# A hybrid mLSTM and sliding-window attention step: an earlier release for the score banks, and another order on VectorE ahead of h

## The chip, the cores and the metric

The kernel runs on one core of a Trainium2 chip. A core has five engines with an instruction stream each: TensorE (PE in the profile, with its weight loads as PEld), VectorE (DVE), ScalarE (ACT), GpSimd (POOL) and SyncE (SP), which here only issues DMAs. They meet by semaphores. The metric is the time of one execution in microseconds, median of several runs.

## What is computed

One layer for 1024 prompt tokens and 8 x 8 sample tokens: an RMS norm, one input projection, two groups of heads beside each other, one output projection, a norm and a residual. Cut to what matters here:

```
proj = rms(x, g_pre) @ w_in            # split into qa ka va za | qm km vm om zm ig fg
# attention: 8 query heads, 2 key heads of 64, window 128, a sink per head
s = einsum(qa, ka) * 64**-0.5 + bias
p = softmax(concatenate([s, sink]))[..., :-1]
a_out = einsum(p, va) * silu(za)
# mLSTM: 4 heads of 128, chunks of 128 tokens; D and g are exponentials of the gates
S = einsum(qm, km) * D
num = einsum(S, vm) + g * einsum(qm, C)
den = sum(S) + g * einsum(qm, n)
h = num / maximum(abs(den), exp(-m))
C, n = decay * C + einsum(w, km, vm), decay * n + einsum(w, km)
m_out = sigmoid(om) * rms(h, g_mh) * silu(zm)
y = x + rms(concatenate([a_out, m_out]) @ w_out, g_post)
```

## The kernel before

All operands are fp32; the large products are split into a high and a low part, so that one sub-tile of the input projection is 24 matmuls (8 slices of the inner dimension, three products each, L551). The projection has 25 tiles of 128 output columns (`ka`, four each of `qa`, `km`, `qm`, `za`, `om`, `zm`), each cut into three sub-tiles of 368, 368 and 352 tokens: 75 sub-tiles. They use two PSUM banks in turn. ACT evacuates each (`evac`), and after some of them splits the next weight tile: `w_hi` on ACT, then `w_lo` on POOL (attention) or DVE (mLSTM).

The small work is laid between the sub-tiles by hand. Every engine runs the same loops, `it` counting the sub-tile, and the order within an iteration is the order of the code. There is no scheduler.

**Attention stage** (24 iterations, the sub-tiles of `km` and `qm`). Unit `u` is half of the heads of one block of 128 queries, u = 0 to 15; unit 16 is all sample tokens. In iteration `it` PE computes `scores(it)` (32 matmuls, L602, into banks 0 and 1), then 24 matmuls of the projection, and in odd iterations `values((it - 3) // 2)` (L628), for which it waits for `pT_done`. DVE does `denominators(it - 1)`, `band_transpose(it - 2)` (writes `pT`, L1253) and `score(it)`: L1227 reads the two banks, scales and adds the bias and writes `prob`; L1238 to L1241 take the row maxima, put in the sink, negate, and write `sd`, which lets semaphore `scored` go up. ACT waits for `scored` and takes the exponentials of `prob` (L954), then evacuates the sub-tile. POOL multiplies by `rden` (L1523), ahead of the transpose. `step` is a helper: its instruction raises `dve_step`, and DVE waits for that before it issues the next.

**mLSTM stage** (12 iterations, the sub-tiles of `za`). Unit 0 is the sample tokens, units 1 to 8 are the prompt's chunks. PE in iteration `it`: `h_transposes(it - 2)` (L749), `numerator(it - 1)` and `state_update(it - 1)` (L702 to L714), 7 matmuls of the projection, `m_scores(it)` (L678), `sample_inter`, 7 matmuls, `sample_round` (L738), `k_transposes(it)` (L687), 10 matmuls. `h_transposes` waits for both `h_done` and `sd_done`. DVE: the mask `DT` (L1285), `hT_evac` (L1372), `h_denominator`, `state`, `inter_second` in even iterations, `h_mean_square` (L1357, L1358), `h_scale` (L1364, writes `hs`), `q_gate` (L1293, `qmT` times the exponentials `Gt`, both in SBUF), `sd_mul` (L1276, the scores in PSUM times `DT`, writes `SD`), the split `w_lo` in every third iteration, and the update of the sample state `Cs`. Between L1358 and L1364 POOL computes the factor `hf` in three small operations (L1553, L1484 with a power of -0.5, L1555) and then `vmk` (L1545).

Of the kernel before, what the change touches and what calls it, by code (L numbers as in the profile page):

```python
# [22 lines left out]
ALU = mybir.AluOpType  # L23
# [11 lines left out]
AH, KVH, HD = 8, 2, 64  # L35
# [9 lines left out]
BAND = WIN + PQ  # L45
# [56 lines left out]
def build(nc, i, o):  # L102
# [12 lines left out]
    def sb(name, shape, dt, offset):  # L115
        return nc.alloc_sbuf_tensor_at(name, shape, dt, offset=offset)
# [19 lines left out]
    k = [at["K"]]  # L136
# [52 lines left out]
    bias_0 = sb("bias_0", [P, AH, BAND], F32, GI + 10496)  # L189
    kcT = sb("kcT", [P, DEC_B, KEYS_S], F32, GI + 10496)  # L190
    vc = sb("vc", [P, DEC_B, KV_W], F32, GI + 14848)
    bias_p = sb("bias_p", [P, AH, BAND], F32, GI + 18944)
# [56 lines left out]
    ps = nc.alloc_psum_tensor("ps", [P, 8, 512], F32)  # L249
    sems = {}  # L250

    def s(name):
        if name not in sems:
            sems[name] = nc.alloc_semaphore(name)
        return sems[name]
# [12 lines left out]
    def wait(eng, name, value):  # L268

        if value > 0:  # L270
            eng.wait_ge(s(name), value)
# [26 lines left out]
    def unit_tokens(u):  # L298

        return (NC, T_P, T_S) if u == 0 else (u - 1, P * (u - 1), P)  # L300
# [181 lines left out]
    def _(pe):  # L482
# [91 lines left out]
        for c in range(NTILE):  # L574
            _, n = x_cols(c)
            last = nc.tensor.transpose(ps[0:PQ + MH, c // 4, (c % 4) * P:(c % 4) * P + n], gates[0:n, c, 0:PQ + MH], ident[0:n, 0:n])
# [9 lines left out]


        def scores(u):
            wait(pe, "scored", u)
            if u == 0:  # L590
                wait(pe, "proj_free", S_P2 - 2)
                wait(pe, "cols_done", 1)
            if u < 2 * NC:
                blk, pair = u // 2, u % 2
                if u == 0:
                    wait(pe, "kpad_ready", 1)
                for g in range(2):
                    for kv in range(KVH):
                        rows = slice(kv * HD, (kv + 1) * HD)
                        for a in range(4):  # L600
                            q0 = blk * P + PQ * a
                            last = mm(ps[PQ * a:PQ * (a + 1), kv, g * BAND:(g + 1) * BAND], qaT[rows, 2 * pair + g, q0:q0 + PQ],  # L602
                                      kaT_pad[rows, q0:q0 + BAND], start=True, stop=True)
            else:
                wait(pe, "qs_ready", 1)
                pe.wait_ge(s("kc_ld"), 32)
                for b in range(DEC_B):
                    r = 32 * (b % 4)
                    for kv in range(KVH):
                        rows = slice(kv * HD, (kv + 1) * HD)  # L610
                        last = mm(ps[r:r + 32, kv, (b // 4) * KEYS_S:(b // 4 + 1) * KEYS_S], qs[rows, b, :], kcT[rows, b, :],
                                  start=True, stop=True)
            last.then_inc(s("qk_done"), 1)
# [478 lines left out]
    def _(dve):  # L1092
        V = nc.vector
        step = Step(dve, "dve_step")
        TT, TS, STT, CP = V.tensor_tensor, V.tensor_scalar, V.scalar_tensor_tensor, V.tensor_copy
# [85 lines left out]
        for dst, bias, q in ((ib, bgi, 0), (fb, bgf, PQ)):  # L1181
            last = TS(dst[:], ps[q:q + MH, 0:3, :].rearrange("p b t -> p (b t)")[:, 0:T], bias[q:q + MH, 0:1], None, ALU.add)
# [11 lines left out]
        for b in range(DEC_B):  # L1194
            c0 = T_P + DEC_T * b
            last = V.tensor_tensor_scan(out=rd[:, c0:c0 + DEC_T], data0=rc[:, c0:c0 + DEC_T], data1=ib[:, c0:c0 + DEC_T],
                                        initial=m0T[:, b:b + 1], op0=ALU.add, op1=ALU.max)
# [19 lines left out]
        def score(u):  # L1217

            wait(dve, "qk_done", u + 1)
            wait(dve, "pT_done", u - 1)  # L1220
            b = u % 2
            if u == 0:
                dve.wait_ge(s("bias_ld"), 48)
            if u < 2 * NC:
                heads = slice(4 * (u % 2), 4 * (u % 2) + 4)
                p = prob[:, b, :, :]
                step(STT(out=p.rearrange("p (v g) k -> p v g k", v=KVH), in0=ps[:, 0:2, 0:2 * BAND].rearrange("p v (g k) -> p v g k", g=2),  # L1227
                         scalar=float(HD) ** -0.5, in1=(bias_0 if u < 2 else bias_p)[:, heads, :].rearrange("p (v g) k -> p v g k", v=KVH),
                         op0=ALU.mult, op1=ALU.add))
                sink = sink_p[:, heads]  # L1230
            else:
                for kv in range(KVH):
                    last = STT(out=prob_s[:, 2 * kv:2 * kv + 2, :], in0=ps[:, kv, 0:2 * KEYS_S].rearrange("p (a k) -> p a k", a=2),
                               scalar=float(HD) ** -0.5, in1=bias_s[:, kv:kv + 1, :].broadcast_to([P, 2, KEYS_S]),
                               op0=ALU.mult, op1=ALU.add)
                step(last)
                p, sink = prob_s[:], sink_s[:]
            step(V.tensor_reduce(mx[:, b, :], p, AX_X, ALU.max))  # L1238
            step(TT(mx[:, b, :], mx[:, b, :], sink, ALU.max))  # L1239
            TS(nmx[:, b, :], mx[:, b, :], -1.0, None, ALU.mult)  # L1240
            TT(sd[:, b, :], sink, mx[:, b, :], ALU.subtract).then_inc(s("scored"), 1)  # L1241
# [29 lines left out]
        def sd_mul(u):  # L1271
            _, _, n = unit_tokens(u)
            wait(dve, "d_done", u + 1)
            wait(dve, "s_done", u + 1)
            wait(dve, "num_done", u - 1)
            TT((SD if u else SDs)[0:n, :, :], ps[0:n, 1, 0:MH * n].rearrange("p (h t) -> p h t", h=MH), DT[0:n, :, 0:n], ALU.mult)\  # L1276
                .then_inc(s("sd_done"), 1)

        def mask_weights(u):
            _, _, n = unit_tokens(u)  # L1280
            dve.wait_ge(s(f"r_ld{u % 3}"), 32 if u == 0 else 16 * (u // 3 + (2 if u % 3 == 0 else 1)))
            wait(dve, "kw_done", u)
            m = causal if u else causal_s
            r1 = Gt[:, u % 3, :, :] if u else Gt[0:T_S, 0, 2:4, :].rearrange("p a (h t) -> p (a h) t", t=T_S)
            TT(DT[0:n, :, 0:n], r1, m[:].unsqueeze(1).broadcast_to([n, MH, n]), ALU.min).then_inc(s("mask_done"), 1)  # L1285
# [45 lines left out]
        def inter_second(r):  # L1331
            wait(dve, "it_done", r + 1)
            wait(dve, "it_evac", r)
            part = ITs[:, r // 2, :]
            STT(out=part, in0=ps[:, 4, IT0:IT0 + W1], scalar=inter_msk[:, 1:2], in1=part, op0=ALU.mult, op1=ALU.add)\
                .then_inc(s("it_evac"), 1)

        def num_view(n):
            return ps[0:n, 2:4, 0:2 * W1].rearrange("p b (h v) -> p b h v", v=W1)
# [20 lines left out]
        def h_scale(u):  # L1360
            _, _, n = unit_tokens(u)
            v = H_ORDER.index(u) + 1
            wait(dve, "hf_ready", v)
            TT(hs[0:n, :, :].rearrange("p (b h) v -> p b h v", b=2), num_view(n)[:, :, :, 0:MD],  # L1364
               hf[0:n, :].rearrange("p (b h) -> p b h", b=2).unsqueeze(3).broadcast_to([n, 2, 2, MD]), ALU.mult)\
                .then_inc(s("h_done"), 1)

        def hT_evac(u):
            _, off, n = unit_tokens(u)
            v = H_ORDER.index(u) + 1  # L1370
            wait(dve, "hT_done", v)
            TT(qmT[:, :, off:off + n], ps[:, 1, 0:MH * n].rearrange("p (h t) -> p h t", h=MH),  # L1372
               gmh[:].unsqueeze(2).broadcast_to([P, MH, n]), ALU.mult).then_inc(s("hT_evac"), 1)

        def splits(sub):
            for n in PLAN.get(sub, []):
                split_lo(dve, V, n)

        for it in range(S_P4 - S_P3):
            if it <= NC:  # L1380
                mask_weights(it)
            if it >= 3:
                hT_evac(it - 2 if it <= NC + 2 else 0)
            done = None
            if 2 <= it <= NC + 2:
                done = it - 1 if it <= NC + 1 else 0
                h_denominator(done)
            if 2 <= it <= NC + 1:
                state(it - 1)
            if 1 <= it <= N_ROUND and it % 2 == 0:  # L1390
                inter_second(it - 1)
            if done is not None:
                h_mean_square(done)
                h_scale(done)
            if it <= NC:
                q_gate(it)
                sd_mul(it)
            if it == 0:
                sample_extras()
            if it >= 1:  # L1400
                splits(S_P3 + it - 1)
            if 1 <= it <= N_ROUND:
                sample_state(it - 1)
            if it < N_ROUND:
                sample_n(it)
# [56 lines left out]
        p = NTILE - 1  # L1462
# [7 lines left out]
        for q in range(2):  # L1470
            wait(dve, "yg_done", q + 1)
            STT(out=ys[q], in0=ys[q], scalar=stat[:, NTILE + p:NTILE + p + 1], in1=x_res[:, p % 2, 512 * q:512 * (q + 1)],
                op0=ALU.mult, op1=ALU.add).then_inc(s("y_ready"), 1)
# [208 lines left out]
```

## Time and profile before

| | us |
|---|---|
| median of 3 runs (573.79 to 574.02) | 573.85 |
| the profiled execution | 573.66 |
| its span in the trace | 571.8 |
| PE busy | 550.1 |
| DVE busy | 249.3 |
| ACT busy | 200.0 |
| POOL busy | 132.9 |
| idle time of PE in 148 to 262 us, put down to DVE | 1.9 |
| idle time of PE in 262 to 375 us, ahead of L749 | 1.7 |

The span runs from the first to the last recorded instruction; the execution is some 1.9 us longer. In the rows further down a timeline line gives start, duration, engine, line of the kernel, operation, output and inputs, the number of instructions merged, and in brackets the idle time of that engine just before and the instruction that ended it. The stages by time: norm, transposes and token-major projection up to about 85 us, gates and first tiles to 148, attention to 262, mLSTM to 375, gates and the rest of the projection, then the output projection from about 470.

### The profile page before, as it was taken

How to read it: one execution, taken by the hardware profiler on the slowest of the kernel's cores; microseconds unless marked ns; L12 is line 12 of the kernel's file. 1: busy time of each engine (PE TensorE's matmuls, PEld its weight loads, DVE VectorE, ACT ScalarE, POOL GpSimd, SP SyncE). 2: the span in 40 equal slices, each digit the busy share in tenths (PEclk: the TensorE clock that was granted, in tenths of full speed). 3: DMA queues.
4: the chain of work that ended last, by engine and by line, in shares of the span. 5: the costliest groups of instructions: out<-in, count | busy, mean ns of one | idle time of the engine just before them, and what ended most of it. 6: DMA issues, size and time to landing. Idle time of an engine off the chain costs nothing.

```text
span 571.8 us, 10440 instructions
## 1 busy us (share of the span) xinstructions
PE 550.1 (96%) x4354; PEld 507.0 (89%) x4354; DVE 249.3 (44%) x468; ACT 200.0 (35%) x542; POOL 132.9 (23%) x148
## 2 busy tenths in 40 slices
PE   2999999999999999999999999999999999999996
PEld 2999999999988889899888888899999998888874
DVE  3743214910456666611366757335324327052223
ACT  3352223223354545432565464244332224011011
POOL 3511021112323434331112121235422220011001
PEclk9999999999999999999999999999999999999999
DMA  8422006131142122014233320411122315044231
GB/s 312 147 76 91 1 2 211 77 112 38 38 134 62 62 63 83 6 36 105 64 93 112 89 79 20 111 49 63 37 75 77 108 37 185 0 148 147 102 101 55
DMA packets 34166, 48.72 MB, mean 85 GB/s; under 512 B 3888, under 2 KB 25456, under 8 KB 34104
## 3 DMA queue, kind: packets, MB, share of 16 engines
q1 hardware_dynamic: 25544, 43.80, 23.5%
q10 hardware_dynamic: 8576, 4.26, 2.9%
q8 instruction: 34, 0.56, 0.4%
q14 instruction: 12, 0.10, 0.1%
HBM read 40.48 MB, written 8.56 MB: 86 GB/s over the span
## 4 chain that ended last, share of the span: by engine, by line
PE 74%; DVE 14%; ACT 6%; DMA 2%; issue 2%; POOL 1%; SPq 0%; ACTq 0%; DVEq 0%; POOLq 0%
PE ps L551 37%; PE ps L490 8%; PE ps L491 8%; PE ps L492 8%; ACT prob L954 4%; DVE mx L1238 2%; DVE prob L1227 2%; DVE pT L1253 2%; PE ps L510 1%; PE ps L702 1%; DVE mx L1239 1%; DMA g_pre_b<-in_g_pre 1%; PE ps L714 1%; PE ps L704 1%; PE ps L495 1%
## 5 line engine op out<-in xcount | busy, mean ns | idle before, releaser
L551 PE MATMUL ps<-x_hl,w_hi 128*128 128x368 f32 (+1 forms) x1200 | 300.0, 330 | 0.8 <-ACT qaT L887 0.6
L551 PEld LDWEIGHTS ps<-x_hl,w_hi 128*128 128x128 f32 x1200 | 210.0, 188 | 7.5 <-issue 5.9
L551 PE MATMUL ps<-x_hl,w_lo 128*128 128x368 f32 (+1 forms) x600 | 197.0, 328 | 0.0
L551 PEld LDWEIGHTS ps<-x_hl,w_lo 128*128 128x128 f32 x600 | 112.7, 188 | 0.1
L329 POOL TENSOR_TENSOR w_lo<-w_raw,w_hi 128x1024 fp32r<-128x1024 f32 x14 | 33.7, 2406 | 86.1 <-ACT w_hi L864 86.1
L490 PE MATMUL ps<-wt_hi,x_hl 128*128 128x324 f32 x128 | 41.8, 327 | 1.6 <-DVE x_hl L1114 1.4
L954 ACT ACTIVATE prob<-prob,nmx 128x160 f32<-128x160 f32 x64 | 26.6, 417 | 46.6 <-DVE sd L1241 46.6
L492 PE MATMUL ps<-wt_hi,x_hl 128*128 128x324 f32 x128 | 40.8, 318 | 0.0
L491 PE MATMUL ps<-wt_lo,x_hl 128*128 128x324 f32 x128 | 40.7, 318 | 0.0
L1573 POOL TENSOR_TENSOR qmT<-qmT,sg 128x368 f32<-128x368 f32 (+1 forms) x24 | 25.0, 1041 | 57.8 <-DVE sg L1426 36.4
L1523 POOL TENSOR_TENSOR prob<-prob,rden 128x640 f32<-128x640 f32 x16 | 20.1, 1254 | 63.8 <-DVE rden L1247 63.8
L877 ACT ACTIVATE sg<-ps 128x368 f32<-128x368 f32 (+1 forms) x24 | 11.4, 474 | 63.6 <-PE ps L551 63.6
L1456 DVE SCALAR_TENSOR_TENSOR y_out<-ps,stat,g_post_b 128x1024 f32<-128x1024 f32 x7 | 9.0, 1283 | 50.2 <-POOL stat L1484 50.2
L864 ACT ACTIVATE w_hi<-w_raw 128x1024 fp32r<-128x1024 f32 x25 | 26.3, 1051 | 12.0 <-DMA w_raw<-in_w_in_tiles 12.0
L1088 ACT ACTIVATE junk<-ps 128x1024 f32<-128x1024 f32 x7 | 7.2, 1026 | 60.0 <-PE ps L492 60.0
L490 PEld LDWEIGHTS ps<-wt_hi,x_hl 128*128 128x128 f32 x128 | 25.1, 196 | 2.6 <-DVE x_hl L1114 1.8
L490 PE MATMUL ps<-wah,a_hl 128*128 128x512 f32 x64 | 25.3, 395 | 0.0
L491 PE MATMUL ps<-wal,a_hl 128*128 128x512 f32 x64 | 25.3, 395 | 0.0
L492 PE MATMUL ps<-wah,a_hl 128*128 128x512 f32 x64 | 25.3, 395 | 0.0
L491 PEld LDWEIGHTS ps<-wt_lo,x_hl 128*128 128x128 f32 x128 | 25.0, 195 | 0.0
L491 PE MATMUL ps<-wbl,m_hl 128*128 128x512 f32 x64 | 25.0, 390 | 0.0
L490 PE MATMUL ps<-wbh,m_hl 128*128 128x512 f32 x64 | 24.9, 390 | 0.0
(221 smaller groups left out, 802.9 us busy)
## 6 DMA issues: line engine op xcount, KB each, us to landing
w_raw<-in_w_in_tiles SPq DMA_DIRECT2D x25, 512.0 KB, 3.6
x_raw<-in_x_prompt SPq DMA_DIRECT2D x8, 512.0 KB, 3.9
w_raw<-in_w_out_tiles SPq DMA_DIRECT2D x8, 512.0 KB, 3.3
x_res<-in_x_prompt SPq DMA_DIRECT2D x8, 512.0 KB, 4.4
out_y_prompt<-y_out SPq DMA_DIRECT2D x7, 512.0 KB, 2.9
wt_raw<-in_w_tok SPq DMA_DIRECT2D x4, 648.0 KB, 10.5
Cs<-in_state_C SPq DMA_DIRECT2D x16, 128.0 KB, 2.3
Gt<-r_rows ACTq DMA_DIRECT2D x8, 256.0 KB, 3.5
```

Source lines behind the costliest of these rows:

```text
L329: engine.tensor_tensor(lo[:, q, :], w_raw[:, n % 2, :], hi[:, q, :].bitcast(F32), ALU.subtract).then_inc(s("w_lo"), 1)
L490: mm(out, hl[:, 0, :], wh, start=first, stop=False, skip_group_check=True)
L491: mm(out, hl[:, 0, :], wl, start=False, stop=False, skip_group_check=True)
L492: return mm(out, hl[:, 1, :], wh, start=False, stop=final, skip_group_check=True)
L551: last = mm(ps[:, 6 + sub % 2, 0:w], wt, xt, start=(at_ == 0), stop=(at_ == 23))
L864: A_(dst, w_raw[:, n % 2, :], ACT.Copy).then_inc(s("w_hi"), 1)
L954: A_(p, p, ACT.Exp, bias=nmx[:, b, g:g + 1], accum_out=den[:, b, g:g + 1])
L1227: step(STT(out=p.rearrange("p (v g) k -> p v g k", v=KVH), in0=ps[:, 0:2, 0:2 * BAND].rearrange("p v (g k) -> p v g k", g=2), scalar=float ...
L1238: step(V.tensor_reduce(mx[:, b, :], p, AX_X, ALU.max))
L1253: V.transpose(pT[:, blk % 2, :, 2 * pair:2 * pair + 2, :], prob[:, u % 2, :, :].rearrange("p (v g) k -> p v g k", v=KVH))\
L1523: Q.tensor_tensor(p, p, rden[:, b, :].unsqueeze(2).broadcast_to([P, G, BAND]), ALU.mult)\
L1573: Q.tensor_tensor(x, x, sg[:, m % 2, 0:w], ALU.mult).then_inc(s("sg_used"), 1)
```

## The change

Two edits. First, DVE raises a new semaphore, `sc_read`, when the instruction that reads the two score banks is done; PE's `scores(u)` waits for `sc_read` where it waited for `scored`. DVE itself waits for `sc_read` ahead of its reduction, where it waited for its step. ACT still waits for `scored`. Second, in the mLSTM stage `q_gate(it)` and `sd_mul(it)` stand ahead of `h_scale(done)`.

```diff
         def scores(u):
-            wait(pe, "scored", u)
+            wait(pe, "sc_read", u)
...
             if u < 2 * NC:
...
-                step(STT(out=p.rearrange("p (v g) k -> p v g k", v=KVH), in0=ps[:, 0:2, 0:2 * BAND].rearrange("p v (g k) -> p v g k", g=2),
-                         scalar=float(HD) ** -0.5, in1=(bias_0 if u < 2 else bias_p)[:, heads, :].rearrange("p (v g) k -> p v g k", v=KVH),
-                         op0=ALU.mult, op1=ALU.add))
+                STT(out=p.rearrange("p (v g) k -> p v g k", v=KVH), in0=ps[:, 0:2, 0:2 * BAND].rearrange("p v (g k) -> p v g k", g=2),
+                    scalar=float(HD) ** -0.5, in1=(bias_0 if u < 2 else bias_p)[:, heads, :].rearrange("p (v g) k -> p v g k", v=KVH),
+                    op0=ALU.mult, op1=ALU.add).then_inc(s("sc_read"), 1)
                 sink = sink_p[:, heads]
             else:
...
-                step(last)
+                last.then_inc(s("sc_read"), 1)
                 p, sink = prob_s[:], sink_s[:]
+            wait(dve, "sc_read", u + 1)
             step(V.tensor_reduce(mx[:, b, :], p, AX_X, ALU.max))
...
                 h_mean_square(done)
-                h_scale(done)
             if it <= NC:
                 q_gate(it)
                 sd_mul(it)
+            if done is not None:
+                h_scale(done)
```

PE around `scores(15)`, the last prompt unit, before:

```order
L551 MATMUL ps<-x_hl,w_hi 128x352 x2
L551 MATMUL ps<-x_hl,w_lo 128x352
L602 MATMUL ps<-kaT_pad,qaT 32x160 [waits scored]
L602 MATMUL ps<-kaT_pad,qaT 32x160 x15
L551 MATMUL ps<-x_hl,w_hi 128x368 [waits w_lo,proj_free]
L551 MATMUL ps<-x_hl,w_hi 128x368
```

and after:

```order
L551 MATMUL ps<-x_hl,w_hi 128x352 x2
L551 MATMUL ps<-x_hl,w_lo 128x352
L602 MATMUL ps<-kaT_pad,qaT 32x160 [waits sc_read]
L602 MATMUL ps<-kaT_pad,qaT 32x160 x15
L551 MATMUL ps<-x_hl,w_hi 128x368 [waits w_lo,proj_free]
L551 MATMUL ps<-x_hl,w_hi 128x368
```

No instruction of PE moved; the one wait has another name.

DVE in iteration 2 of the mLSTM stage (the other iterations up to 8 alike), before:

```order
L1357 SCALAR_TENSOR_TENSOR hf<-hss,hrd 128x4 [waits sq_done]
L1358 TENSOR_TENSOR hf<-hf,hrd 128x4 [waits dve_step]
L1364 TENSOR_TENSOR hs<-ps,hf 128x512 [waits hf_ready]
L1293 TENSOR_TENSOR qmT<-qmT,Gt 128x4x128 [waits s_done,g_done]
L1276 TENSOR_TENSOR SD<-ps,DT 128x512 [waits num_done,s_done,d_done]
L1322 SCALAR_TENSOR_TENSOR Cs<-Cs,dec_s,ps 128x129 [waits rcup_done,cn_ready]
```

and after, where the lines from 1236 on have numbers one higher:

```order
L1358 SCALAR_TENSOR_TENSOR hf<-hss,hrd 128x4 [waits sq_done]
L1359 TENSOR_TENSOR hf<-hf,hrd 128x4 [waits dve_step]
L1294 TENSOR_TENSOR qmT<-qmT,Gt 128x4x128 [waits s_done,g_done]
L1277 TENSOR_TENSOR SD<-ps,DT 128x512 [waits num_done,s_done,d_done]
L1365 TENSOR_TENSOR hs<-ps,hf 128x512 [waits hf_ready]
L1323 SCALAR_TENSOR_TENSOR Cs<-Cs,dec_s,ps 128x129 [waits rcup_done,cn_ready]
```

`hs`, with its wait for POOL's `hf_ready`, moved behind two operations that don't wait for POOL.

## Rows read from the trace of the kernel before

**Rows 1.** The page: busy time by engine, and granted clock in 40 slices.

```profile
PE 550.1 (96%) x4354; PEld 507.0 (89%) x4354; DVE 249.3 (44%) x468; ACT 200.0 (35%) x542; POOL 132.9 (23%) x148
...
PEclk9999999999999999999999999999999999999999
```

**Rows 2.** Waits, 148 to 262 us: total us, times, longest; PE and weight loads.

```profile
PE ps L602 <- DVE sd L1241: 1.9, 4, 0.6
...
PEld ps L602 <- DVE sd L1241: 3.8, 7, 0.9
```

**Rows 3.** Waits, 262 to 375 us, PE.

```profile
PE ps L749 <- issue: 1.2, 3, 0.5
PE ps L749 <- DVE SD L1276: 0.5, 1, 0.5
```

**Rows 4.** Timeline: start, us, engine, line, operation; attention unit 2, then PE's scores.

```profile
160.76 0.81 DVE L1227 SCALAR_TENSOR_TENSOR prob<-ps,bias_p 128x640 f32<-128x640 f32 x1
...
162.74 0.15 DVE L1241 TENSOR_TENSOR sd<-sink_p,mx 128x4 f32<-128x4 f32 x1
...
162.95 0.78 PE L602 MATMUL ps<-kaT_pad,qaT 64*32 64x160 f32 x32 [0.62 <-DVE sd L1241]
```

**Rows 5.** Timeline: attention unit 14 on DVE, and PE's scores of unit 15.

```profile
228.41 0.82 DVE L1227 SCALAR_TENSOR_TENSOR prob<-ps,bias_p 128x640 f32<-128x640 f32 x1
...
230.61 0.78 PE L602 MATMUL ps<-kaT_pad,qaT 64*32 64x160 f32 x32 [0.40 <-DVE sd L1241]
```

**Rows 6.** Timeline: the last band transpose on DVE, and PE's last block of values.

```profile
244.23 0.83 DVE L1253 STREAM_TRANSPOSE pT<-prob 128x640 f32<-128x640 f32 x1
...
245.55 1.44 PE L628 MATMUL ps<-pT,va_w 32*64 32x128 f32 x80
```

**Rows 7.** Timeline: mLSTM iteration 2, from k-transposes to h-transposes.

```profile
291.27 0.16 DVE L1358 TENSOR_TENSOR hf<-hf,hrd 128x4 f32<-128x4 f32 x1
...
291.52 0.23 POOL L1553 TENSOR_SCALAR hf<-hf 128x4 f32<-128x4 f32 x1 [6.96 <-DVE hf L1358]
...
291.83 1.04 POOL L1484 TENSOR_TENSOR hf<-hf,minus_half 128x4 f32<-128x4 f32 x1
...
292.44 0.66 PE L687 MATMUL ps<-ident,kmT 128*128 128x128 f32 x4
...
292.95 0.20 POOL L1555 TENSOR_TENSOR hf<-hf,hrd 128x4 f32<-128x4 f32 x1
...
293.10 0.61 POOL L1545 TENSOR_TENSOR vmk<-vm,seqsel 64x258 f32<-64x258 f32 x1
...
293.18 0.69 DVE L1364 TENSOR_TENSOR hs<-ps,hf 128x512 f32<-128x512 f32 x1 [1.76 <-POOL hf L1555]
...
293.79 0.68 DVE L1293 TENSOR_TENSOR qmT<-qmT,Gt 128x512 f32<-128x512 f32 x1
...
294.39 0.69 DVE L1276 TENSOR_TENSOR SD<-ps,DT 128x512 f32<-128x512 f32 x1
...
295.22 0.63 PE L749 MATMUL ps<-ident,hs 128*128 128x128 f32 x4 [0.54 <-DVE SD L1276]
```

**Rows 8.** Timeline: the same two places of PE in iteration 3.

```profile
302.89 0.66 PE L687 MATMUL ps<-ident,kmT 128*128 128x128 f32 x4
...
305.06 0.60 PE L749 MATMUL ps<-ident,hs 128*128 128x128 f32 x4
```

**Rows 9.** Timeline: the same in iteration 8, the last of the seven.

```profile
353.40 0.66 PE L687 MATMUL ps<-ident,kmT 128*128 128x128 f32 x4
...
356.18 0.63 PE L749 MATMUL ps<-ident,hs 128*128 128x128 f32 x4 [0.54 <-issue]
```

**Rows 10.** Timeline: POOL and DVE beside each other, ahead of the mLSTM stage and in it.

```profile
267.47 2.39 POOL L329 TENSOR_TENSOR w_lo<-w_raw,w_hi 128x1024 fp32r<-128x1024 f32 x1 [12.36 <-ACT w_hi L864]
...
267.66 2.48 DVE L1285 TENSOR_TENSOR DT<-Gt,causal_s 64x256 f32<-64x256 f32 x1 [14.87 <-DMA Gt<-r_rows]
...
275.71 0.86 POOL L1545 TENSOR_TENSOR vmk<-vm,seqsel 64x258 f32<-64x258 f32 x1 [5.85 <-ACT Gt L990]
```

## The prediction, made before the changed kernel ran

> **What bounds the kernel now.** I read four views, in this order. The page first: TensorE (PE) is busy for 550.1 of 571.8 us and its granted clock stands at 9 tenths or more in every slice, that is the 2.4 GHz level throughout [rows 1]. So what an edit on another engine can give back is only the time in which PE stands still. Then the waits of PE, by stage. In the attention stage (148 to 262 us) the matmuls of the scores, L602, waited four times on DVE's `sd`, 1.9 us in all; the weight loads ahead of them seven times, 3.8 us [rows 2]. In the mLSTM stage (262 to 375 us) the transposes of h, L749, waited 1.7 us in four places, once put down to `SD` and three times to nothing that the profile shows [rows 3]. From 375 us on PE waits for nobody. Third, the timeline around these waits, to see which event lets PE go. Fourth, the same timeline one step further on: what PE would meet next if the wait were gone.
>
> A warning on sizes: the idle time of a PE row leaves out the tail of the matmul before it, so it is smaller than what the wait costs. I take the cost from intervals between starts, waited against not waited.
>
> **Part 1, the scores.** Nothing is added on DVE: the wait of L1238 on its own engine's count becomes a wait on `sc_read`, same instruction, same place. On PE the event is earlier. Unit 2 shows it: the multiply-add that reads the banks runs from 160.76 to 161.57, `sd` ends at 162.89, and PE starts at 162.95, 0.06 after `sd` [rows 4]. The three small operations and the reduction lie between. With the change PE could start at 161.63.
>
> How much of it stays? DVE and ACT run a loop of their own: scores, exp on ACT, denominators, transpose, next scores. No step of it waits for PE after unit 1, so it keeps its times when PE's waits go. Unit 14 is the last at which PE waited: banks read at 229.23, PE at 230.61 [rows 5]. If PE meets only the banks there, it starts at 229.29, 1.32 us earlier. Earlier units free PE more but are caught up by this point, since PE can't pass that event. But the next place to look is the last block of values. It waits for `pT` of unit 15, which DVE writes only after the denominators of the sample unit, in the loop. That transpose ran from 244.23 to 245.06, and the values started at 245.55 [rows 6]. PE moved by 1.32 would be there at 244.23 and would wait until 245.13 (0.06 as above, and a little for the start). What is left of the 1.32 is 245.55 - 245.13 = **0.42 us**. This wait in the changed kernel is new: 0.9 us at L628, with the projection's next 24 matmuls queued behind it; nobody but ACT's evacuation waits for those. The bounds of this part: 0 below (a later event of the same loop can't be later than now) and 3.8 above, all that the weight loads waited [rows 2]. I take 0.42 since its two rows stand in the trace.
>
> **Part 2, the order on DVE in the mLSTM stage.** In iterations 2 to 8 DVE computed `hf` (L1358), idled until GpSimd (POOL) had done its three small operations, scaled h, gated the queries, multiplied `SD`. PE's transposes L749 wait for both `h_done` and `sd_done`, and `sd_done` came last. Iteration 2: L1358 ends at 291.43; POOL's three run from 291.52 to 293.15; `hs` 293.18 to 293.87; `qmT` from 293.79; `SD` 294.39 to 295.08; PE at 295.22 [rows 7]. So four of the waits of [rows 3] are one and the same, although the profile names only one: the others start 0.10 us after `SD` ends, too.
>
> Moved: `qmT` and `SD` (0.68 each, overlapping by 0.08, together 1.29 us) go into the idle 1.75 us. Both have their inputs by then: ACT's exponentials and PE's m_scores were over before L1357. Nothing is added and no DMA moves. New times: `qmT` 291.37 to 292.05, `SD` to 292.65, `hs` when POOL is ready, 293.18 to 293.87. PE then needs 293.87 plus 0.10, that is 293.97, where before it needed 295.18.
>
> What PE's own work needs: from the start of the k-transposes L687 to L749 there are ten matmuls of the projection. Where nothing was late this took 305.06 - 302.89 = 2.17 us (tiles of 368 columns) [rows 8]; with 352 columns, sixteen fewer at 2.4 GHz or 6.7 ns a matmul, it is 2.10. In the seven iterations the intervals are 2.78, 2.17, 2.47, 2.76, 2.49, 2.19 and 2.78 us (first [rows 7], last [rows 9]); tiles of 352 columns are in the first, fourth and last. Over the need: 0.68 + 0 + 0.30 + 0.66 + 0.32 + 0.02 + 0.68 = **2.66 us**. In the first, PE alone would be at L749 at 294.54; the new event is at 293.97, so 0.57 us of cover is left. In the iterations after a `w_lo` of DVE the split now comes behind `hs` and ahead of the sample update as before, so the update and the mask behind it start 1.2 us earlier, not later. If the cover is used up, PE pays what is over it, seven times.
>
> What could eat the cover is POOL. Its `vmk` ran beside DVE's `hs`, which reads PSUM, and neither was longer than elsewhere (0.61 and 0.69) [rows 7]. But a DVE operation with two SBUF inputs, `DT`, started 0.19 after POOL's `w_lo` and ended only at 270.14, 0.28 after it: 2.48 us instead of 0.69 [rows 10]. `qmT` has two SBUF inputs, and now it lies on POOL's three operations. `SD` reads PSUM as `hs` does. `qmT` comes first, at 291.37 against 291.52, so POOL may start up to 0.53 late and `hs` end at 294.40, PE free at 294.50: still not past 294.54. I take the cover as just holding. The Trainium skill, SBUF — State Buffer, section Who interferes with whom, has this as a rule: a DVE instruction with two SBUF inputs contends with a GpSimd instruction that reads SBUF, and whichever starts first has the shared ports for the whole instruction. The trace agrees for `DT`. By that rule POOL waits out `qmT`, as just worked out, and `SD` costs it nothing; without any such contention the sum would be the same.
>
> **Sum.** 0.42 + 2.66 = 3.1 us. What follows (projection, gates, output projection) hangs on PE: before 375 us the weight tiles are loaded and split a tile ahead, and every load there is let go by an evacuation that moves with PE. So I expect it to arrive at the end whole. The profiled execution took 573.66 us (span 571.8 and 1.9 around it), which makes 570.55; against the median of 573.85 it is 570.75, and I say **570.7**.
>
> **Rivals.**
> - PE isn't held at the last values (the wait has slack that I misread). Then the 1.32 us stay: 573.85 - 1.32 - 2.66 = 569.9. For it: nobody waited on `pT` so far. Against it: the two rows of [rows 6]. 5%.
> - POOL's pow is first at the ports and `qmT` waits for it. The pow ends at 292.87 [rows 7]; then `qmT` 0.68, `SD` 0.60, `hs` 0.69 more: 294.8, PE at 294.9 instead of 295.22. The gain is 0.3 in each of five iterations, 1.5, with part 1 1.9 us: 571.9. Against it: DVE is 0.15 us ahead. 13%. The rule of the page quoted above allows this too, if the start order is the other one.
> - The wait only changes its name. If `SD` as well as `qmT` kept POOL off, POOL would start at 292.65, `hs` end at 295.0, and PE start within 0.1 us of now. Only part 1 is left: 573.4. For it: the chain of POOL is 1.63 us long and the idle time was all POOL's. Against: `hs` with its PSUM input beside `vmk`. 10%.
> - Slower. As the last, and POOL loses time again at each of its three operations while DVE goes on to the sample update. POOL's first `vmk`, issued beside a `qmT`, took 0.86 us where the next took 0.61 [rows 7, 10]. A loss of 0.25 us for each of the three would put `hs` 0.7 us past the old end of `SD`, in seven iterations: +4.9 - 0.4, 578.3. It decides from the point where POOL is late by more than 1.2 us an iteration; the most that [rows 10] support is one operation of 0.68. 4%.
> - The forecast, 68%.
>
> **How the numbers follow.** The likeliest gives 570.7. The first two rivals lie at 569.9 and 571.9; with their own spread of 0.2 to 0.4 the range is 569.7 to 572.3, and leaves out the last two, 14%. A measurement of this kernel can tell about 0.2% from no change, 1.15 us: faster is below 572.7. Faster: 68 + 5 + 13 = 86%; same 10%; slower 4%.
>
> **What would show it.** Right: no L602 waits on DVE; L628 of the last block waits about 0.9 us for `pT` and starts 0.4 earlier; L687 to L749 takes 2.1 to 2.2 us in all seven iterations; `hs` still has idle time ahead of it, of about 0.5 instead of 1.75 us; from 375 us on everything is 3.1 us earlier. Wrong: L628 unwaited (first rival); `qmT` longer than 1 us (second); POOL's three operations starting after 292.6 in iteration 2 (third, fourth); or a wait after 375 us that wasn't there.

## The result, and the profile after

| | before | after |
|---|---|---|
| median of 6 runs, us | 573.88 | 570.25 |
| lowest and highest | 572.77, 574.44 | 569.42, 570.96 |
| the profiled execution | 573.66 | 569.42 |
| its span | 571.8 | 567.6 |

The changed kernel takes 0.9938 of the time before (95% interval 0.9925 to 0.995), 3.6 us less. The forecast was 570.7, with a range of 569.7 to 572.3.

The two profiled executions differ by 4.2 us, and not all of that is the change. At the very start PE waits for the first block of `x` (L510): 9.5 us before, 8.3 after. By the first scores, ahead of every line that was edited, the kernel after is 0.77 us early. So I measure from PE's first scores (L602) to the last of the seven h-transposes that the prediction counts (L749, behind the k-transposes of iteration 8; below, an iteration is named by its k-transposes L687). This stretch took 208.50 us before (147.68 to 356.18) and 205.06 after (146.91 to 351.97): **3.44 us less**. From 375 us on PE waits for nobody, as before, and nothing is given back. This stretch is also the measure in the expectations below.

What answers to [rows 1], on the page of the kernel after:

```profile
PE 548.4 (97%) x4354; PEld 506.7 (89%) x4354; DVE 248.9 (44%) x468; ACT 199.9 (35%) x542; POOL 135.7 (24%) x148
```

The same instructions, and POOL busy for 2.8 us more. Something on POOL got longer: what, stands further down.

The waits of PE, attention stage (148 to 262 us), where [rows 2] had four on `sd`. Columns: engine, output and line that waited, what ended the wait, total us, times, longest:

```profile
PE ps L628 <- DVE pT L1254: 0.8, 1, 0.8
PE ps L602 <- DVE prob L1227: 0.7, 2, 0.4
```

And in the mLSTM stage (262 to 375 us), where [rows 3] had 1.7 us ahead of L749:

```profile
PE ps L738 <- ACT ITs L1037: 0.3, 1, 0.3
```

No scores wait for `sd` any more. Two still wait for the read of the banks, and the last block of values waits for `pT`, which it did not before. All waits of L749 are gone. The one at L738 belongs to iteration 1, was there before as well, and the second edit doesn't reach it.

The timeline of the kernel after, units 2 and 14 and the last transpose, which answers to [rows 4 to 6]. Columns: start, us, engine, line, operation, output and inputs, count, and in brackets the idle time before with what ended it:

```profile
160.01 0.81 DVE L1227 SCALAR_TENSOR_TENSOR prob<-ps,bias_p 128x640 f32<-128x640 f32 x1
...
161.49 0.77 PE L602 MATMUL ps<-kaT_pad,qaT 64*32 64x160 f32 x32
...
227.65 0.82 DVE L1227 SCALAR_TENSOR_TENSOR prob<-ps,bias_p 128x640 f32<-128x640 f32 x1
...
228.53 0.78 PE L602 MATMUL ps<-kaT_pad,qaT 64*32 64x160 f32 x32 [0.45 <-DVE prob L1227]
...
243.49 0.83 DVE L1254 STREAM_TRANSPOSE pT<-prob 128x640 f32<-128x640 f32 x1
...
244.38 1.43 PE L628 MATMUL ps<-pT,va_w 32*64 32x128 f32 x80 [0.83 <-DVE pT L1254]
```

In unit 2 PE starts its scores 0.67 us after DVE's read has ended (160.82), unhindered. In unit 14 the read ends at 228.47 and PE starts 0.06 later. At the values PE stands for 0.83 us and starts 0.06 after the transpose. Against the start of the stretch the values come at 97.47 us after, 97.87 before: 0.40 earlier.

Iteration 2 of the mLSTM stage after, with the rows of [rows 7] in their new order:

```profile
290.09 0.16 DVE L1359 TENSOR_TENSOR hf<-hf,hrd 128x4 f32<-128x4 f32 x1
290.17 0.69 DVE L1294 TENSOR_TENSOR qmT<-qmT,Gt 128x512 f32<-128x512 f32 x1
290.34 0.61 POOL L1555 TENSOR_SCALAR hf<-hf 128x4 f32<-128x4 f32 x1 [6.96 <-DVE hf L1359]
...
290.78 0.68 DVE L1277 TENSOR_TENSOR SD<-ps,DT 128x512 f32<-128x512 f32 x1
291.03 1.04 POOL L1486 TENSOR_TENSOR hf<-hf,minus_half 128x4 f32<-128x4 f32 x1
291.22 0.65 PE L687 MATMUL ps<-ident,kmT 128*128 128x128 f32 x4
292.16 0.20 POOL L1557 TENSOR_TENSOR hf<-hf,hrd 128x4 f32<-128x4 f32 x1
...
292.39 0.69 DVE L1365 TENSOR_TENSOR hs<-ps,hf 128x512 f32<-128x512 f32 x1 [0.93 <-POOL hf L1557]
```

`qmT` and `SD` now lie in the time in which DVE had nothing to do, of which 0.93 us is left instead of 1.76. POOL's first operation, begun beside `qmT`, takes 0.61 us instead of 0.23, and `hs` ends at 293.08. PE starts L749 at 293.30. The seven intervals from L687 to L749 are now 2.08, 2.18, 2.19, 2.16, 2.17, 2.19 and 2.08 us, 15.05 in all; before they made 17.64.

### The profile page after: what moved, and what is told of

Read it like the earlier page. It is cut to its first block, busy times and chain, and to the rows that moved or that the text cites. A ratio compares the mean times of both kernels' runs of the same rounds, so it can differ in the third digit from the quotient of the medians.

```text
span 567.6 us, 10440 instructions
## 1 busy us (share of the span) xinstructions
PE 548.4 (97%) x4354; PEld 506.7 (89%) x4354; DVE 248.9 (44%) x468; ACT 199.9 (35%) x542; POOL 135.7 (24%) x148
## 4 chain that ended last, share of the span: by engine, by line
PE 74%; DVE 15%; ACT 6%; DMA 2%; issue 1%; POOL 0%; SPq 0%; ACTq 0%; DVEq 0%; POOLq 0%
PE ps L551 36%; PE ps L490 8%; PE ps L492 8%; PE ps L491 8%; ACT prob L954 4%; DVE mx L1239 2%; DVE pT L1254 2%; DVE prob L1227 2%; DVE mx L1240 2%; PE ps L702 2%; PE ps L510 1%; PE ps L714 1%; PE ps L678 1%; PE ps L704 1%; PE ps L495 1%
## 5 line engine op out<-in xcount | busy, mean ns | idle before, releaser
L490 PE MATMUL ps<-wbh,m_hl 128*128 128x512 f32 x64 | 24.9, 390 | 0.0
L492 PE MATMUL ps<-wbh,m_hl 128*128 128x512 f32 x64 | 24.9, 389 | 0.0
```

The costliest lines, as they stand in the source:

```text
L490: mm(out, hl[:, 0, :], wh, start=first, stop=False, skip_group_check=True)
L492: return mm(out, hl[:, 1, :], wh, start=False, stop=final, skip_group_check=True)
```

## The experiments

Ten kernels. The theory was that each edit takes a wait of PE away and the next event of the same engines catches PE, at the places that the prediction named. The rivals were that the new wait at the last values costs nothing, that POOL's operations and DVE's keep each other off, and that the order of `qmT` and `SD` decides. Ratios are to the kernel before on the same chip, whose medians were 573.40 (first four), 573.49 (next four) and 574.06 (last two).

### Each edit alone

The first edit alone, the kernel after with DVE's old order:

```diff
+            if done is not None:
+                h_scale(done)
             if it <= NC:
                 q_gate(it)
                 sd_mul(it)
-            if done is not None:
-                h_scale(done)
```

> Only the first edit: the scores wait for sc_read, DVE keeps its old order in the mLSTM stage. I measure on PE's timeline from the first scores (L602) to the last h-transposes of iteration 8 (L749): 208.50 us in the kernel before (147.68 to 356.18), 205.06 in the changed one (146.91 to 351.97). Theory (the last values wait for a transpose in the DVE/ACT loop, so most of the gain is handed back): 208.1 us, L628 of the last block waits 0.8 us on pT, time 0.4 us under before. Rival (the edit is worth its whole 1.3 us and the second edit less): 207.2 us. The intervals from L687 to L749 in the mLSTM stage stay at 2.78, 2.17, 2.47, 2.76, 2.49, 2.19, 2.78.

Measured: 208.23 us for the stretch, 573.16 in all (ratio 0.9997, 0.9988 to 1.0006). PE's waits in attention are those of the kernel after, and ahead of L749 it waits as in [rows 3], by nearly the same amounts:

```profile
PE ps L749 <- issue: 1.2, 3, 0.5
PE ps L749 <- DVE SD L1277: 0.6, 1, 0.6
```

The values come 97.53 us after the first scores, 0.34 earlier than before. The rival, in which the 1.3 us stay, is out. The timed ratio can't tell 0.3 us from nothing; only the trace does, and there is one trace of each kernel. How far one can be trusted shows in the next run: its code up to the last values is the old one, and they come at 97.98 us, 0.11 later than in the kernel before.

The second edit alone: PE waits for `scored`, DVE's read is a `step` again.

```diff
         def scores(u):
-            wait(pe, "sc_read", u)
+            wait(pe, "scored", u)
```

> Only the second edit: q_gate and sd_mul ahead of h_scale, the scores wait for scored as before. Theory: from the first scores to the last h-transposes 208.50 - 3.02 = 205.5 us, time 3.0 us under before; the seven intervals L687 to L749 as in the changed kernel, 2.08 to 2.19. Rival (the two edits help each other, since PE comes to the mLSTM stage earlier): above 206 us.

Measured: 205.62 us, 570.90 in all (0.9955, 0.9941 to 0.9968). PE's waits, attention and then mLSTM:

```profile
PE ps L602 <- DVE sd L1241: 2.0, 4, 0.6
...
PE ps L738 <- ACT ITs L1037: 0.3, 1, 0.3
```

The waits on `sd` are back, and those of L749 are gone. The edits alone give 0.27 and 2.88 us, 3.15 together, where the change gives 3.44: they add, within some 0.3 us. Nearly all is the order on DVE: by the trace 2.88 us, by the medians 2.5, where I expected 3.0.

### What holds the values

If the last values are held by the DVE and ACT loop, an earlier transpose ought to hand the rest of the 1.32 us back. In the kernel after, the last band transpose goes ahead of the denominators. The old order had also made sure that ACT's evacuation of the block before was over when the values reach its banks; now PE waits for that itself.

```diff
         def values(blk):
             wait(pe, "pT_done", 2 * (blk + 1))
-            wait(pe, "att_out", blk - 1)
+            wait(pe, "att_out", blk)
...
         for it in range(S_P3 - S_P2):
+            if it == 2 * NC + 1:
+                band_transpose(it - 2)
             if 1 <= it <= N_ATT:
                 denominators(it - 1)
-            if 2 <= it <= 2 * NC + 1:
+            if 2 <= it <= 2 * NC:
                 band_transpose(it - 2)
```

> The changed kernel with one more step: in iteration 17 alone DVE does the last band transpose ahead of the denominators of the sample unit (and PE's values wait for the evacuation of the block before, which was ordered by the old place of the transpose). Theory: the 0.83 us that L628 waited goes, from the first scores to the last h-transposes 205.06 - 0.85 = 204.2 us, time 0.8 us under the changed kernel. Rival (PE is held by something else right behind, such as the evacuation of the values or the sample transposes): 205.0 us.

Measured: 204.25 us, 569.17 in all (0.9929, 0.9917 to 0.9942). The timeline:

```profile
242.32 0.84 DVE L1254 STREAM_TRANSPOSE pT<-prob 128x640 f32<-128x640 f32 x1
...
244.24 0.16 DVE L1247 TENSOR_TENSOR den<-den,sd 128x4 f32<-128x4 f32 x1 [1.09 <-ACT sd L955]
...
244.48 1.43 PE L628 MATMUL ps<-pT,va_w 32*64 32x128 f32 x80
```

The transpose ends 1.3 us ahead of the values, which wait for nobody and come 96.61 us after the first scores, 0.86 earlier than in the kernel after; the stretch is 0.81 shorter. So the hand-back at L628 is real, and that is its size.

The row of the denominators shows more: DVE stands for 1.09 us until ACT has taken the exponential of the sink. So it does in every unit from 160 us on. The same exchange in every iteration:

```diff
         for it in range(S_P3 - S_P2):
-            if 1 <= it <= N_ATT:
-                denominators(it - 1)
             if 2 <= it <= 2 * NC + 1:
                 band_transpose(it - 2)
+            if 1 <= it <= N_ATT:
+                denominators(it - 1)
```

(the wait for `att_out` as above)

> As the kernel before this one in the list, but in all iterations: the band transpose lies in the 1.9 us in which DVE waits for ACT's exponentials. Theory (the loop of DVE and ACT, not PE's wait on sd, sets the pace): one turn of the loop gets 0.8 us shorter, 4.5 instead of 5.3 us, less than PE's 4.7 to 6.3; no wait of L602 on DVE is left. From the first scores to the last h-transposes 205.06 - 0.94 - 0.85 = 203.3 us, time 1.8 us under the changed kernel. Rival (transposes beside ACT's and POOL's work on the same tile slow them, or the transpose then waits for POOL): loop stays at 5.3, 204.2 us or more.

Measured: 203.19 us, 568.50 in all (0.992, 0.9907 to 0.9934). Its timeline from about 193 us:

```profile
193.41 0.84 DVE L1254 STREAM_TRANSPOSE pT<-prob 128x640 f32<-128x640 f32 x1
...
195.17 0.78 PE L602 MATMUL ps<-kaT_pad,qaT 64*32 64x160 f32 x32
...
195.41 0.17 DVE L1247 TENSOR_TENSOR den<-den,sd 128x4 f32<-128x4 f32 x1 [1.17 <-ACT sd L955]
...
196.05 0.82 DVE L1227 SCALAR_TENSOR_TENSOR prob<-ps,bias_p 128x640 f32<-128x640 f32 x1 [0.26 <-PE ps L602]
```

The transpose lies under ACT's exponentials. DVE's own waits from 160 to 233 us, the kernel after:

```profile
DVE den L1247 <- ACT sd L955: 25.0, 13, 1.9
```

and this one:

```profile
DVE den L1247 <- ACT sd L955: 15.2, 13, 1.2
DVE prob L1227 <- PE ps L602: 8.5, 11, 1.8
```

In the kernel after, DVE waited 1.9 us a unit for ACT and never for PE in this window. Now it waits for PE in eleven units: the loop of DVE and ACT is shorter than PE's, and PE sets the pace. From the first scores to the last values 95.61 us are left, 1.86 less than in the kernel after.

If so, the first edit should be worth nothing beside this order. The same exchange in the kernel before, with neither edit:

> The kernel before, neither edit, but with the band transpose ahead of the denominators in all iterations. Theory (the loop of DVE and ACT is what PE waited for, and the name of PE's wait matters only as long as the loop is longer than PE's own work): no L602 waits although the scores still wait for sd, and none of L628 either; from the first scores to the last h-transposes 208.50 - 2.3 = 206.2 us, the mLSTM intervals as in the kernel before. Rival (PE needs the earlier event in any case, since sd comes 1.1 us after the banks are read): L602 still waits, 207 us or more.

Measured: 206.24 us, 571.46 in all (0.9966, 0.9953 to 0.9979). PE has no wait at all in the attention stage, and the values come at 95.60 us, as in the kernel with the first edit and this order (95.61). In the mLSTM stage the waits of L749 stand as they were. Once the loop is shorter than PE's work, what PE waits for inside it doesn't matter.

### What the order on VectorE does

The multiply of the scores put back behind `hs`, so that only the queries are gated ahead:

```diff
             if it <= NC:
                 q_gate(it)
-                sd_mul(it)
             if done is not None:
                 h_scale(done)
+            if it <= NC:
+                sd_mul(it)
```

> The changed kernel with sd_mul back behind h_scale: only q_gate lies in the idle time ahead of hs. Theory (PE is let go by the last of hs and SD, plus 0.1 us): SD ends 0.6 us after hs; in iterations 2 and 8 the interval L687 to L749 grows by 0.5 from 2.08, in 5 by 0.2, in 4 and 6 by 0.1 at most; first scores to last h-transposes 205.06 + 1.2 = 206.3 us. Rival (the gain came from q_gate alone, as POOL's delay behind it is the limit now): 205.1 us.

Measured: 206.70 us, 571.91 in all (0.9976, 0.9966 to 0.9985), 0.4 over the expectation. Iteration 2:

```profile
292.98 0.69 DVE L1365 TENSOR_TENSOR hs<-ps,hf 128x512 f32<-128x512 f32 x1 [1.53 <-POOL hf L1558]
293.59 0.68 DVE L1277 TENSOR_TENSOR SD<-ps,DT 128x512 f32<-128x512 f32 x1
294.42 0.63 PE L749 MATMUL ps<-ident,hs 128*128 128x128 f32 x4 [0.36 <-DVE SD L1277]
```

PE waits for `SD` again, in fewer iterations and for less. The seven intervals make 16.37 us: gating the queries ahead gives 1.27 of the 2.59, the multiply the other 1.32. Half a move gives half the gain, since the 0.6 us of `SD` stand behind `hs` again, at the end of the chain. The 0.4 over the expectation lie mostly behind the intervals: the stretches from L749 to PE's state updates L714 make 13.62 us instead of the 13.32 of the kernel after, a term that comes back in part 2 below.

The two exchanged, so that POOL's first operation runs beside `SD`, which reads PSUM, and POOL's pow starts ahead of `qmT`, which has both inputs in SBUF:

```diff
             if it <= NC:
-                q_gate(it)
                 sd_mul(it)
+                q_gate(it)
```

> The changed kernel with sd_mul ahead of q_gate. Theory (two SBUF inputs against POOL, whoever starts first keeps the other out; SD, which reads PSUM, keeps nobody out): POOL's first small operation is back at 0.23 instead of 0.61 us, the pow starts at once, and q_gate, issued during the pow, ends only after it: its row 1.5 us or longer instead of 0.69. POOL's third operation may then wait for q_gate. PE: 205.1 to 205.6 us from the first scores to the last h-transposes. Rival (SD delays POOL as q_gate does, it is only the time that DVE is busy): POOL's first operation stays at 0.6 us and q_gate at 0.7.

Measured: 204.86 us, just under the expected range, and one run of 570.02. Iteration 2:

```profile
290.61 0.69 DVE L1277 TENSOR_TENSOR SD<-ps,DT 128x512 f32<-128x512 f32 x1
290.75 0.23 POOL L1555 TENSOR_SCALAR hf<-hf 128x4 f32<-128x4 f32 x1 [5.93 <-DVE hf L1359]
291.06 1.04 POOL L1486 TENSOR_TENSOR hf<-hf,minus_half 128x4 f32<-128x4 f32 x1
291.22 0.68 DVE L1294 TENSOR_TENSOR qmT<-qmT,Gt 128x512 f32<-128x512 f32 x1
```

This is the start order of the prediction's second rival, made on purpose. Beside `SD` POOL's first operation is 0.23 us long again. `qmT` starts 0.16 us after the pow, inside its 1.04 us, and isn't held at all: 0.68 us. So it is in all seven iterations, where it starts 0.15 to 0.68 into the pow. Nor does it hold `hs`, which still has idle time ahead of it, 0.10 us at the least (iteration 3, where POOL's third operation, begun beside `qmT`, took 0.30 instead of 0.20). The contention of [rows 10] doesn't come with every long operation of POOL. The stretch is 0.2 us shorter than in the kernel after, and that lies in iteration 1 to 2 (L687 to L687 8.42 us instead of 8.61). DVE's `w_lo` was ahead of POOL's `vmk` there and took 1.22 us instead of 1.56, and DVE's copy of the sample sums, for which PE's L714 waits, ended 0.92 us ahead of it, where in the kernel after it ended 0.15 ahead, as wherever PE waits for it.

Last, `hs` behind the split and the update of the sample state, 1.3 us of work, or 2.5 with a split, none of which waits for POOL's three operations:

```diff
-            if done is not None:
-                h_scale(done)
...
             if 1 <= it <= N_ROUND:
                 sample_state(it - 1)
+            if done is not None:
+                h_scale(done)
```

> The changed kernel with h_scale moved on behind the weight split and the sample update, to see how little cover is left. Theory: in iterations without a split hs ends 0.2 to 0.5 us later, the intervals L687 to L749 grow by 0 to 0.3; in iterations 4 and 7, with a split of 1.2 us ahead that may also stand behind POOL's pow, by 1.5 to 2. From the first scores to the last h-transposes 205.06 + 4 = 209 us, slower than the kernel before's 208.50 in this stretch. Rival (0.5 us and more of cover in each iteration): 206.5 us or less.

Measured: 206.48 us, one run of 571.14: the size that I expected is missed by 2.5 us, and the time is the rival's. The row of iteration 4, one of those with a split:

```profile
310.91 1.04 POOL L1486 TENSOR_TENSOR hf<-hf,minus_half 128x4 f32<-128x4 f32 x1
311.25 1.22 DVE L329 TENSOR_TENSOR w_lo<-w_raw,w_hi 128x1024 fp32r<-128x1024 f32 x1
...
312.02 0.51 POOL L1557 TENSOR_TENSOR hf<-hf,hrd 128x4 f32<-128x4 f32 x1
...
313.62 0.68 DVE L1365 TENSOR_TENSOR hs<-ps,hf 128x512 f32<-128x512 f32 x1
314.35 0.66 PE L749 MATMUL ps<-ident,hs 128*128 128x128 f32 x4 [0.62 <-DVE hs L1365]
```

The intervals are 2.37, 2.16, 2.97, 2.17, 2.16, 2.19 and 2.16: only iterations 2 and 4 pay, 0.29 and 0.79 against the kernel after. Most of the update fits into the 0.93 us of idle time, the pow again holds nothing (`w_lo` 1.22 us, as elsewhere; it is POOL's third operation that pays, 0.51 instead of 0.20, and no one waits for that here), and in the odd iterations, in which DVE has no `inter_second`, POOL's first operation begins 1.1 to 1.9 us earlier against L687 than in the even ones, so that not even the split of iteration 7 is felt. The steps that failed were to charge each iteration with the same cover, and to let the pow hold the split. The rival has the time but not the mechanism: iteration 2 has no 0.5 us of cover.

### The best of both

The kernel after with the transposes first and the multiply first:

> The changed kernel with both orders that measured well: the band transposes ahead of the denominators in all iterations, and sd_mul ahead of q_gate. Theory (they lie in different stages and add): from the first scores to the last h-transposes 203.19 - 0.2 = 203.0 us, 568.4 us, 1% under the kernel before. Rival (the 0.2 us of the second order was chance): 203.2 us.

Measured: 203.02 us, 568.63 in all (0.9904, 0.9888 to 0.9921). The step from iteration 1 to 2 is 8.41 us again, but 0.2 us is too little for the medians. And the transposes first with the second edit alone, PE waiting for `scored` as before:

> The band transposes first and the mLSTM order of the changed kernel, but PE's scores wait for scored again. Theory (with the shorter loop sd is always there in time, so that the first edit is worth nothing): from the first scores to the last h-transposes 203.2 us as with it, no wait of L602. Rival (the earlier event still buys something): 203.5 us or more.

Measured: 203.25 us, 568.54 in all (0.9904, 0.9889 to 0.9918). PE has no wait in the attention stage. With the transposes first, the kernel with the early release (203.19) and the one without it (203.25) are the same. The three versions at 568.5 to 568.6 beat both kernels, by 4.9 to 5.5 us against before on the same chip, and by 1.6 to 1.8 against the median of after, which was not taken beside them. The stretch says 1.8 to 2.0. The last of the three shows that they don't need the first edit.

## Why the prediction was right, point by point

**What bounds.** PE set the time, and only its standing still could be won. Confirmed: with the edits the waits went, and the time followed.

**Part 1.** Worked out as 0.42 us, of 1.32 at L602 of unit 15. Measured to the last values: 0.40 in the kernel after, 0.34 with the edit alone, with some 0.1 us of doubt for a single trace. The new wait at L628 was put at 0.9 and is 0.83 on the row. That it is this wait that gives the rest back was only argued from [rows 6]; the run with the last transpose first shows it, since there 0.86 come back.

One sentence of this part was wrong in its words: no wait of L602 on DVE, it said under what would show it. Two of them remain, 0.7 us, on the read of the banks, and the sum had reckoned with just that in unit 15. It costs nothing beyond the 1.32 already counted.

**Part 2.** Worked out as 2.66 us. The term itself, L687 to L749, gave 17.64 - 15.05 = 2.59. From the last values to the last L749 the kernel after is 3.04 us shorter, however, so 0.45 was missing from the sum. Of this, 0.34 lie in the six stretches that follow a wait, from L749 to L714: 13.66 before, 13.32 after. The largest piece, 0.20, is the one behind iteration 4. Before:

```profile
315.19 0.63 PE L749 MATMUL ps<-ident,hs 128*128 128x128 f32 x4
...
317.29 0.17 DVE L1325 COPY n_s<-Cs 128x4 f32<-128x4 f32 x1
...
317.61 1.13 PE L714 MATMUL ps<-vm,kw 128*128 128x129 f32 x8
```

After:

```profile
312.97 0.60 PE L749 MATMUL ps<-ident,hs 128*128 128x128 f32 x4
...
314.54 0.17 DVE L1326 COPY n_s<-Cs 128x4 f32<-128x4 f32 x1
...
315.19 1.06 PE L714 MATMUL ps<-vm,kw 128*128 128x129 f32 x8
```

PE's L714 waits for DVE's copy of the sample sums, too. The row doesn't show it as idle time, but before, this copy ended at 317.46 and PE began 0.15 later, as it does each time that the copy comes last; after, it ends 0.48 us ahead of PE. `hs` and the update behind it moved forward by what `qmT` and `SD` had taken, and the prediction said so ("the update and the mask behind it start 1.2 us earlier"), but gave it no price. The rest is 0.03 in most of the others: a PE that comes out of a wait takes that much longer over the transposes (0.63 against 0.60). Some 0.1 us is spread over the other stretches in pieces of 0.05 and less, and stays unassigned.

**The cover.** Forecast as 0.57 us without contention, 0.04 if POOL's first operation waits out `qmT`. It does: 0.61 us instead of 0.23, and in the median of nine at that (a view of one line, before and then after; ns, min, median, max):

```profile
L1553 POOL TENSOR_SCALAR hf<-hf x9: 221/228/231, 291.5 to 369.9; 128x4 f32<-128x4 f32 x8, 64x4 f32<-64x4 f32 x1
```

```profile
L1555 POOL TENSOR_SCALAR hf<-hf x9: 222/608/610, 290.3 to 365.6; 128x4 f32<-128x4 f32 x8, 64x4 f32<-64x4 f32 x1
```

This costs 0.38, not 0.53: POOL starts at once and its operation ends 0.09 after `qmT`. With 0.10 for PE to follow `hs` (293.08), the cover in iteration 2 is 293.30 - 293.18 = 0.12 us. It was indeed just enough there, and that is the smallest. The sign given for the idle time ahead of `hs`, about 0.5 us, was reckoned without this hold; it is 0.93, since `hs` itself came 0.39 later after L1359 than before.

Iteration 7 is the exception, and a useful one: POOL's first operation was 0.02 us ahead of `qmT`, and it was the pow, issued into the running `qmT`, that paid, 1.31 us instead of 1.04.

```profile
337.95 0.72 DVE L1294 TENSOR_TENSOR qmT<-qmT,Gt 128x512 f32<-128x512 f32 x1
338.25 1.31 POOL L1486 TENSOR_TENSOR hf<-hf,minus_half 128x4 f32<-128x4 f32 x1
```

Six times 0.38 and this 0.27 are 2.55 of the 2.8 us by which POOL got busier. The cover of iteration 7 is large enough that PE feels nothing of it. In iteration 5 the interval L687 to L749 is 2.16 instead of 2.08, but `hs` ended at 322.09 and PE came at 322.69: PE's own matmuls followed each other a little more slowly, so this is no wait, and it makes the 2.59 of part 2 smaller than the 2.66 forecast.

**The rivals.** PE not held at L628: out, the wait is there. POOL's pow first, with `qmT` behind it: `qmT` was ahead of the pow in all seven iterations, as forecast, and where I forced the other order, `qmT` wasn't held. This rival was given 13% on the strength of [rows 10] and had no mechanism here. The size read from those rows was off, too: the prediction set 2.48 us beside 0.69, which is the mask of 128x512. The 64x256 one takes 0.42 where it starts ahead of POOL's `w_lo` (the run with the first edit alone). Names only change, and slower: both rest on `SD` keeping POOL off. It doesn't: beside it, the pow has its 1.04 us.

The Trainium skill, SBUF — State Buffer, section SBUF: two separate sides, states that of a GpSimd instruction and a DVE one with two SBUF inputs, the one that starts first has the shared ports for its whole length and the other is blocked. For `qmT` ahead of POOL's first operation the trace agrees, 0.61 against 0.23 us. For the pow ahead of `qmT` and of `w_lo` it doesn't: 0.68 and 1.22 us, no longer than alone. The measurement decides.

**The total.** 0.42 + 2.66 was 3.1; the stretch gave 0.40 + 3.04 = 3.44, and the medians 3.6 with an interval of about 0.7 to either side. The forecast of 570.7 was too slow by 0.45, which is about the size of what part 2 left out. With an interval of 0.7 that near match is luck; it is the stretch, 3.44 against 3.08, that shows the sum 0.36 short.

## What to carry to other kernels

When a wait of the bounding engine goes, walk on to the next event of the same helpers before booking the gain: here 1.32 us shrank to 0.40 within one loop, and moving one transpose in that loop under the other engine's work won more than the earlier release, and made it needless. An operation that waits for another engine should stand behind work that doesn't, as long as the idle time ahead of it is longer than that work; what stands behind the pair moves forward with it, and if the bounding engine waits for that too, it belongs in the sum. Measure such an edit between two marks inside the kernel, since the first scores came anywhere from 146.91 to 148.31 us in the twelve traces, by code that no edit touched.

## What the runs showed of the hardware

Which operations of VectorE and GpSimd hold each other depends on more than who was first and how many inputs lie in SBUF. GpSimd's plain operation on 128x4 behind a two-input `qmT`: 0.61 instead of 0.23 us. `qmT` behind GpSimd's pow on 128x4 (1.04 us): 0.68, not held; `w_lo` likewise 1.22. A pow issued 0.30 us into `qmT` took 1.31 instead of 1.04 and ended 0.89 after it. GpSimd's long `w_lo` ahead of `DT` held it to the end, and it finished 0.28 us behind [rows 10]. Two middling ones hurt each other in both orders. In the kernel after `vmk` comes first, and VectorE's split pays:

```profile
282.77 0.61 POOL L1547 TENSOR_TENSOR vmk<-vm,seqsel 64x258 f32<-64x258 f32 x1 [7.37 <-PE ps L738]
...
282.90 1.56 DVE L329 TENSOR_TENSOR w_lo<-w_raw,w_hi 128x1024 fp32r<-128x1024 f32 x1
```

With the multiply first the split was ahead, and `vmk` pays:

```profile
283.13 1.22 DVE L329 TENSOR_TENSOR w_lo<-w_raw,w_hi 128x1024 fp32r<-128x1024 f32 x1
...
283.59 1.23 POOL L1547 TENSOR_TENSOR vmk<-vm,seqsel 64x258 f32<-64x258 f32 x1 [7.63 <-PE ps L738]
```

One reading is that GpSimd holds the ports only while it moves data, which for four elements a partition is a small part of the pow's 1.04 us. The pow of iteration 7 fits: it lost 0.27 us of the 0.42 for which `qmT` still ran. No run measured that by itself, and it stays open.
